# Closing feed-forward, down projection: inner chunks 0 to 7 as four more pairs of seven half products

## What is computed

```python
def swiglu(h, w_gate, w_up, w_down):
    return (jax.nn.silu(h @ w_gate) * (h @ w_up)) @ w_down
...
        h = h + 0.5 * swiglu(rmsnorm(h, ffn2_norm[layer]),
                             ffn2_w_gate[layer], ffn2_w_up[layer], ffn2_w_down[layer])
    return rmsnorm(h, final_norm)
```

## Time and profile before

| | us |
|---|---|
| median of 3 runs | 2114.79 (2113.94 to 2115.39) |
| profiled execution | 2114.31 |
| its span | 2112.5 |
| PE busy in the span | 2100.9 |
| POOL, DVE, ACT busy | 1554.9, 1328.5, 826.3 |

### The profile page before, as it was taken

How to read it: one execution, slowest core, us unless ns; L and a number is a source line. 1 busy time by engine, 2 the same in 40 slices (tenths; PEclk the granted TensorE clock), 3 DMA queues, 4 the chain that set the end, 5 groups by cost and what they waited for, 6 DMA issues and landing times. The chain is left out here.

```text
span 2112.5 us, 36503 instructions
## 1 busy us (share of the span) xinstructions
PE 2100.9 (99%) x13094; PEld 1855.2 (88%) x13094; DVE 1328.5 (63%) x1973; ACT 826.3 (39%) x1570; POOL 1554.9 (74%) x1390
## 2 busy tenths in 40 slices
PE   9999999999999999999999999999999999999998
PEld 7899988888888899998889998886878888999987
DVE  6876796695455577764377666456872746766533
ACT  5255312034223355541245552134362434555312
POOL 7778897667974778888778887785757656788774
PEclk9999999999999999999999999999999999999999
DMA  6333333223331233333223333332322222333332
GB/s 200 114 120 112 100 99 121 90 77 100 125 104 53 95 104 110 106 105 120 93 97 106 112 104 102 98 100 75 105 86 94 80 65 88 112 102 114 100 99 81
DMA packets 115418, 215.05 MB, mean 102 GB/s; under 512 B 12832, under 2 KB 14400, under 8 KB 115008
## 3 DMA queue, kind: packets, MB, share of 16 engines
q1 hardware_dynamic: 111024, 202.03, 29.5%
q10 hardware_dynamic: 4240, 10.99, 1.4%
HBM read 208.77 MB, written 4.19 MB: 101 GB/s over the span
## 5 line engine op out<-in xcount | busy, mean ns | idle before, releaser
L551 POOL TENSOR_TENSOR w_split<-w_raw,w_split 128x512 fp32r<-128x512 f32 (+1 forms) x486 | 671.0, 1381 | 41.3 <-ACT w_split L1834 1.1
L627 PE MATMUL ps<-x,w_split 128*128 128x512 f32 (+1 forms) x1766 | 680.9, 386 | 0.3 <-DVE tg L2248 0.2
L629 PE MATMUL ps<-x,w_split 128*128 128x512 f32 (+1 forms) x1766 | 674.0, 382 | 0.0
L628 PE MATMUL ps<-x,w_split 128*128 128x512 f32 (+1 forms) x1766 | 673.7, 382 | 0.0
L541 POOL TENSOR_SCALAR w_split<-w_raw 128x512 fp32r<-128x512 f32 x482 | 338.0, 701 | 343.5 <-PE ps L629 328.5
L837 PE MATMUL ps<-x,w_split 128*128 128x264 f32 (+1 forms) x1904 | 535.2, 281 | 1.1 <-DVE ps L2351 1.0
L839 PE MATMUL ps<-x,w_split 128*128 128x264 f32 (+1 forms) x1904 | 535.0, 281 | 0.0
L838 PE MATMUL ps<-x,w_split 128*128 128x264 f32 (+1 forms) x1904 | 533.4, 280 | 0.0
L627 PEld LDWEIGHTS ps<-x,w_split 128*128 128x128 f32 x1766 | 331.8, 188 | 74.5 <-issue 9.4
L629 PEld LDWEIGHTS ps<-x,w_split 128*128 128x128 f32 x1766 | 331.9, 188 | 64.6
L628 PEld LDWEIGHTS ps<-x,w_split 128*128 128x128 f32 x1766 | 332.0, 188 | 64.2 <-issue 1.4
(11 more groups left out here) (350 smaller groups left out, 2547.7 us busy)
## 6 DMA issues: line engine op xcount, KB each, us to landing
w_raw<-in_stream SPq DMA_DIRECT2D x758, 256.0 KB, 2.8
arena<-in_memT ACTq DMA_DIRECT2D x2, 1024.0 KB, 5.5
s_tables<-kv ACTq DMA_DIRECT2D x4, 512.0 KB, 3.0
arena<-s_tables ACTq DMA_DIRECT2D x4, 512.0 KB, 4.2
out<-h ACTq DMA_DIRECT2D x6, 256.0 KB, 2.3
h<-in_xT SPq DMA_DIRECT2D x4, 256.0 KB, 5.0
...
```

The costliest lines, as they stand in the source:

```text
L551: pool.tensor_tensor(lo, x, hi.bitcast(F32), ALU.subtract).then_inc(split_ready if half else S("half_split"), 1)
L627: pe.matmul(dst, wh, xh, start=start, stop=False)
L628: pe.matmul(dst, wh, xl, start=False, stop=False)
L629: return pe.matmul(dst, wl, xh, start=False, stop=stop)
```

## The change

Feed-forward 3 gets four more pairs, 22 to 25 (EXTRA = {3: 4}). Pair 22 + j is the product of hidden chunks 0 to 7 with the output tiles 2j and 2j + 1 of the down projection, in the place of a gate and an up tile. The other 14 hidden chunks go through the down projection as before (DOWN_N[3] = 14). The weight stream keeps its 381 blocks; 8 of them are laid out otherwise. The token side of these pairs are hidden chunks: three blocks as they are (A11, and A21 and A22 together in Aa and Ab), and four sums S1, S2, S4, S3, each made in two halves of two chunks, so eight steps (HID_SUMS). In pair 11 + i DVE makes sum i (`hid_add`) and in the next its low part (`hid_sum_low`), ACT its high part (`hid_sum_high`). In pair 21 ACT makes the high parts of A11, Aa and Ab; DVE makes the low parts of A11 and Aa, POOL that of Ab, behind its work for pair 22. DVE adds half of the outputs of these pairs to h at once.

The core of the diff:

```diff
+EXTRA = {3: 4}
+SEVEN_END = {f: FC + EXTRA.get(f, 0) for f in SEVEN}
+SEVEN_BEFORE = {f: sum(SEVEN_END[g] - at for g, at in SEVEN.items() if g < f) for f in range(5)}
+EVICTED_BEFORE = {f: FC * f + sum(n for g, n in EXTRA.items() if g < f) for f in range(5)}
+DOWN_N = {f: FC - 2 * EXTRA.get(f, 0) for f in range(4)}
+HID_SUMS = [f"{name}{u}" for u in "ab" for name in ("S1", "S2", "S4", "S3")]
+HID_PARTS = ["lead"] + HID_SUMS + ["A11", "Aa", "Ab"]
+HID_FROM = 11
...
+            def hid_low(f, name):
+
+                high, src = hid_operand(f, name, 0)
+                pool.wait_ge(S("s_hi"), hid_part(f, name))
+                pool.tensor_tensor(hid_operand(f, name, 1)[0], src, high.bitcast(F32), ALU.subtract
+                                   ).then_inc(S("hid_lo"), 1)
...
-                    for p in range(SEVEN[f], FC):
-                        if p - 2 >= SEVEN[f]:
+                    for p in range(SEVEN[f], SEVEN_END[f]):
+                        if SEVEN[f] <= p - 2 < FC - 2:
                             seven_product(f, p - 2)
+                        if f in EXTRA and p >= FC + 2:
+                            seven_product(f, p - 4)
                         seven_prepare(f, p)
-                    seven_product(f, FC - 2)
-                    b = FFN_AT[f] + 2 * FC
+                        if f in EXTRA and p == FC:
+                            hid_low(f, "Ab")
...
+                if p == FC:
+                    pe.wait_ge(S("s_lo"), hid_lower(f, "A11"))
...
-                with pe.Fori(1, 5) as i:
+                with pe.Fori(1, (nd - 2) // 4) as i:
...
+                def hid_sum_high(i):
+
+                    name, u = HID_SUMS[i][0:2], "ab".index(HID_SUMS[i][2])
+                    act.wait_ge(S("s_sum"), sums_before(f, len(HID_SUMS)) + 4 + i + 1)
+                    act.activation(hid_summed(name, 0, slice(2 * u, 2 * u + 2)), hid_sum, ACT.Copy
+                                   ).then_inc(S("s_hi"), 1)
+
+                def hid_high(name):
+
+                    q = seven_of(f, FC - 1)
+                    act.wait_ge(S("m_done"), 3 * q + (1 if name == "A11" else 3))
+                    dst, src = hid_operand(f, name, 0)
+                    act.activation(dst, src, ACT.Copy).then_inc(S("s_hi"), 1)
+
+                for p in range(at, SEVEN_END[f]):
                     high(p, "T4")
-                    if p > at:
+                    if at < p <= FC:
                         silu((p - 1) // 2, (p - 1) % 2)
-                    more = p + 1 < FC
+                    more = p + 1 < SEVEN_END[f]
                     if p > at:
                         keep(p, "c1")
                     if more:
                         high(p + 1, "B11")
+                    if f in EXTRA and p == HID_FROM - 1:
+                        hid_lead()
+                    if f in EXTRA and HID_FROM <= p < HID_FROM + 8:
+                        hid_sum_high(p - HID_FROM)
                     keep(p, "c5")
+                    if f in EXTRA and p == FC - 1:
+                        hid_high("A11")
                     keep(p, "c2")
+                    if f in EXTRA and p == FC - 1:
+                        hid_high("Aa")
+                        hid_high("Ab")
...
+                    if p >= FC:
+                        out_tile = h[:, 2 * (p - FC) + 1, :]
+                        dve.scalar_tensor_tensor(out_tile, ps[:, BANKS[2 * s + 1], :], 0.5, out_tile, ALU.mult, ALU.add
+                                                 ).then_inc(S("up_ready"), 1)
+                        return
...
+                def hid_add(i):
+
+                    name, u = HID_SUMS[i][0:2], "ab".index(HID_SUMS[i][2])
+                    left, right = {"S1": (hid_quarter(2, 1, u), hid_quarter(2, 2, u)),
+                                   "S2": (hid_sum, hid_quarter(1, 1, u)), "S4": (hid_quarter(1, 2, u), hid_sum),
+                                   "S3": (hid_quarter(1, 1, u), hid_quarter(2, 1, u))}[name]
+                    dve.wait_ge(S("hid_done"), FC * f + 8)
+                    if i:
+                        dve.wait_ge(S("s_lo"), hid_lower(f, HID_SUMS[i - 1]))
+                    dve.tensor_tensor(hid_sum, left, right, ALU.add if name == "S1" else ALU.subtract
+                                      ).then_inc(S("s_sum"), 1)
+
+                def hid_sum_low(i):
+
+                    name, u = HID_SUMS[i][0:2], "ab".index(HID_SUMS[i][2])
+                    chunks = slice(2 * u, 2 * u + 2)
+                    dve.wait_ge(S("s_hi"), hid_part(f, HID_SUMS[i]))
+                    dve.tensor_tensor(hid_summed(name, 1, chunks), hid_sum, hid_summed(name, 0, chunks).bitcast(F32),
+                                      ALU.subtract).then_inc(S("s_lo"), 1)
...
+                def hid_aside(p):
+
+                    if p == HID_FROM:
+                        hid_lead_low()
+                    if HID_FROM < p <= HID_FROM + 8:
+                        hid_sum_low(p - HID_FROM - 1)
+                    if HID_FROM <= p < HID_FROM + 8:
+                        hid_add(p - HID_FROM)
+                    if p == FC:
+                        hid_low("Aa")
```

More of the change, by code:

```diff
@@ L173 @@
 TABLES_BEHIND, SQUARES_BEHIND = (8, 13), 17
-SEVEN_BEFORE = {f: sum(FC - at for g, at in SEVEN.items() if g < f) for f in range(5)}
+EXTRA = {3: 4}
[6 more added lines that the diff above has]
+HID_FROM = 11
 SUMS_AT = {1: "S2", 2: "S4", 3: "S3"}
@@ L253 @@
 A_GAINED = 14 * T
+A_HID = FC * T
 A_QHI = 16 * T
@@ L275, in seven_at, with sums_before @@
     return sorted(SEVEN).index(f)
+def sums_before(f, parts):
+    return 4 * seven_at(f) + sum(parts for g in EXTRA if g < f)
 def is_seven(b):
-    return any(FFN_AT[f] + 2 * at <= b < FFN_AT[f] + 2 * FC for f, at in SEVEN.items())
+    return any(FFN_AT[f] + 2 * at <= b < FFN_AT[f] + 2 * SEVEN_END[f] for f, at in SEVEN.items())
 def sevens_before(b):
@@ L452, in held_chunk, with hid_summed, hid_quarter, hid_operand @@
             return X[1 - NORM_TO[FFN_NORM[f]]][:, SEVEN_HELD[name] + k, part, t]
+        hid_sums = {"S4": kv_r[:].rearrange("p (c s t) -> p c s t", c=4, s=2),
+                    "S1": ar_r[:, A_HID:A_HID + 8 * T].rearrange("p (c s t) -> p c s t", c=4, s=2)}
+        hid_sums["S3"], hid_sums["S2"] = hid_sums["S4"], hid_sums["S1"]
+        hid_sum = ar[:, A_HID + 8 * T:A_HID + 9 * T].rearrange("p (c t) -> p c t", c=2)[:, :, 0:SECOND_T]
+        def hid_summed(name, part, chunks=slice(0, 4)):
+            t = slice(LEAD, FIRST_T) if name in ("S1", "S4") else slice(FIRST_T, T)
+            return hid_sums[name][:, chunks, part, t]
+        def hid_quarter(i, j, u):
+            at = 4 * (j - 1) + 2 * u
+            return hid[:, at:at + 2, FIRST_T if i == 2 else LEAD:T if i == 2 else FIRST_T]
+        def hid_operand(f, name, part):
+            x = NORM_TO[FFN_NORM[f]]
+            if name == "A11":
+                return X[x][:, 0:4, part, 0:FIRST_T], hid[:, 0:4, 0:FIRST_T]
+            at = 4 if name == "Aa" else 6
+            return X[1 - x][:, at:at + 2, part, :], hid[:, at:at + 2, :]
+        def hid_part(f, name):
+            return HID_PARTS.index(name) + 1 + sums_before(f, len(HID_PARTS)) + 4
+        def hid_lower(f, name):
+            return HID_PARTS.index(name) + 1 + sums_before(f, len(HID_PARTS) - 1) + 4
+        def down_chunk(f, d):
+            x = NORM_TO[FFN_NORM[f]]
+            return X[x if f in EXTRA else 1 - x], [6, 7, 4, 5][d % 4]
         block = ctx.enter_context(nc.Block())
@@ L522, in _ @@
                 plain(first, FFN_AT[f] + 2 * SEVEN[f])
-                for p in range(SEVEN[f], FC + 1):
+                for p in range(SEVEN[f], SEVEN_END[f] + 1):
                     seven(f, p)
-                first = FFN_AT[f] + 2 * FC + 2
+                first = FFN_AT[f] + 2 * SEVEN_END[f] + 2
             plain(first, N_BLOCKS)
@@ L1593, in ffn @@
                 else:
-                    with act.Fori(1, 3 if f == 2 else 5) as i:
+                    with act.Fori(d0 // 4 + 1, 3 if f == 2 else 5) as i:
                         for s in range(4):
@@ L2296, in ffn @@
                 else:
-                    with dve.Fori(1, 3 if f == 2 else 5) as i:
+                    with dve.Fori(d0 // 4 + 1, 3 if f == 2 else 5) as i:
                         for s in range(4):
@@ L2410, in seven @@
                 gate((at - 1) // 2, (at - 1) % 2)
-                for p in range(at, FC):
-                    more = p + 1 < FC
+                def hid_add(i):
[8 more added lines that the diff above has]
+                                      ).then_inc(S("s_sum"), 1)
@@ L2416, in seven @@
                     low(p, "T4")
+                    if f in EXTRA:
+                        hid_aside(p)
                     if more:
                         add(p + 1, "T1")
-                    if p == at:
+                    if f in EXTRA and p == FC - 1:
+                        hid_low("A11")
+                        join(p, "C12")
+                        join(p, "C22")
```

(23 more changed lines are left out.)

121 lines of the change are left out of this document (80 added, 41 removed).

## The result

| | before | after |
|---|---|---|
| median, us | 2115.39 (2113.51 to 2116.78, 11 runs) | 2120.02 (2119.31 to 2121.82, 11 runs) |
| profiled execution, us | 2114.31 | 2120.02 |
| its span, us | 2112.5 | 2118.2 |

The ratio is 1.0023, interval 1.0014 to 1.0032: 3.0 to 6.8 us slower, on either side of the 0.2% that a measurement can tell. A second set of runs of the changed kernel (after_again), beside runs of before of its own, gave 1.0023 [1.0014, 1.0032] again. The forecast was 2120.6.

What follows compares the result with a forecast made beforehand. PE, busy 99% of the span, was taken to set the end alone, with any wait added in full. -3.82 (PE's work) + 8.5 (B22) + 1.6 (pair 22) = +6.3 on 2114.3 gave 2120.6 us, own range 2118 to 2123.5.

Steps and rivals of the forecast that it cites:

- PE's work, -3.82: On PE, 8 chunks (43.53 us) go and 4 pairs (39.71 us) come: -3.82 us if PE never waits.
- the estimate: PE's exchange of matmuls by the skill's formula for one matmul alone: 36.8 us for 41.4 us, -4.6 us.
- B22 in pairs 11 to 18, +8.5: PE waits before product B22 for ACT's copy c5: 0.8 us in pair 11, 1.1 in each of 12 to 18.
- the chain: Pairs 11 to 18: DVE's addition waits for POOL's product, ACT's high part and c5 for the addition, B22 for c5.
- Rival A: Pairs 11 to 18: DVE's addition gets in ahead of POOL's product, 0.1 us a pair; 2112.9 us in all, chance 0.17.
- C22 with time to spare: Pairs 11 to 18: DVE's sum C22 ends some 0.8 us before PE's last product needs it, as before.
- Pair 22, +1.6: Copies of hidden chunks and POOL's Ab delay T1's sum; C22 ends at about 10.1, PE wants it at 8.6.
- the prediction's steps for Ab: Pair 22: POOL starts low part Ab at 3.4, about 2.5 us, to 6.9; T1's sum then ends at 7.5.
- they stand ahead of the copies T1, T2, B22, T3, B21, which all slip by some 2.1 us: Pair 21: ACT's three copies of hidden chunks, 3.1 us, delay pair 22's copies by some 2.1 us, and POOL's low parts.
- its base: The forecast adds its +6.3 to 2114.3, the profiled execution of before (2114.31 us); the median is 0.5 above.

Runs made afterwards that it cites:

- e2: Changed kernel, but in pairs 11 to 18 POOL makes the hidden product behind B11's low part, not ahead of it; ratio to before 0.9990 [0.9981, 1.0000].
- e3: Changed kernel, but in pairs 11 to 18 DVE makes the addition first and the sum's low part behind T1's sum; ratio to before 0.9989 [0.9979, 0.9999].
- e1: Changed kernel, but in pairs 11 to 18 ACT makes each hidden sum's high part ahead of copy B21, not c5; ratio to before 0.9999 [0.9989, 1.0008].
- e5: Changed kernel, but in pair 21 ACT's copies Aa and Ab stand behind copies T3 and B21, no longer ahead of T1; one run, 2121.80 us.

## Why the prediction came out

**PE's work, -3.82**: -3.81; the rows' paces held to 0.01. The formula of the Trainium skill's "TensorE: Matmul & The Clock Gate" (Back-to-back issue gap) for a single matmul, by which the estimate was -4.6, is off by 0.8.

**B22 in pairs 11 to 18, +8.5**: +8.34 (0.76 + 7 x 1.083, forecast 0.8 + 7 x 1.1). Each step of the chain stands where it was put. In us from the pair's first matmul (1936.08): product in at 2.11 (forecast 2.12), its end at 3.70 (3.75), the addition's end at 4.23 (4.35), c5's end at 5.16 (5.25), B22 at 5.30 (5.40). The forecast of B22 was late by 0.10, and the 0.08 that the next matmul loses was not in it: two small errors that nearly cancel. e2 and e3 show the cause by taking it away. Rival A was near in its price (0.18 a pair in e2, where the addition gets through; 0.1 forecast) and wrong in its condition: POOL's product does come first.

**C22 with time to spare**: 0.8 us in the forecast. In after it holds; e1 shows that the spare time was there only because B22's wait delayed T4 as well. That sentence was true and less safe than it read.

**Pair 22, +1.6**: +1.69, with the wait and its path as forecast, but the size by luck. T3's low part ends 2.17 into pair 22 (forecast 2.2), Ab holds T1's sum, and C22 is late by it (1.32 us at T4: the step of 1.35 and the 0.08 behind it, less the usual 0.115). The Trainium skill's "SBUF — State Buffer" (SBUF: two separate sides) has the shared port pair held for the whole instruction by whoever starts first; the trace agrees, now for an instruction of that length: T1's sum took 2.45 us and ended 0.56 behind Ab, and came in between where Ab was cut in two.

The luck is in the sum. The prediction lets POOL begin Ab at 3.4, gives it 2.5 us and has it end at 6.9, but 3.4 + 2.5 is 5.9. With 5.9 its own steps bring C22 to 9.1 where PE wants it at 8.6, about +0.6 in the place of +1.6, and the whole to about 2119.6 us, still within its range. In after Ab begins 3.38 into the pair (1991.26 - 1987.88) and ends at 6.75, since it takes 3.37 us. DVE was already at the low part of Aa:

```profile
1990.52 1.86 DVE L2559 TENSOR_TENSOR x<-arena,x 128x1024 fp32r<-128x1024 f32 x1
```

In e5, where Ab came first, it took 2.39. So a slip of 1.0 in the sum stood in for a wait of 0.98 behind an instruction of DVE that the prediction's steps for Ab don't name.

The step "they stand ahead of the copies T1, T2, B22, T3, B21, which all slip by some 2.1 us" was only half of the cause. ACT and DVE by time in pair 21 (from 1977.96) of after:

```profile
1982.74 2.00 ACT L1781 ACTIVATE x<-arena 128x1024 fp32r<-128x1024 f32 x2
1984.63 0.59 ACT L1722 ACTIVATE w_split<-ps 128x512 fp32r<-128x512 f32 x1
...
1985.26 0.42 DVE L2456 TENSOR_TENSOR ps<-ps,sq 128x248 f32<-128x248 f32 x1
1985.59 0.69 DVE L2434 TENSOR_TENSOR ps<-w_raw,ps 128x512 f32<-128x512 f32 x1
```

Behind Aa and Ab T1's copy starts 6.67 in, where it does so 4.79 in in pair 17 of before: a slip of 1.88. It ends at 1985.22, and T2's sum, which in before starts 0.13 behind that copy, could have begun at 1985.35. But on DVE it stands behind C22 and begins at 1985.59, a slip of 2.12. Two causes end 0.24 us apart. Either alone would make nearly all of the slip: e5 shows it for DVE's order; for the copies alone it is worked out from these rows, and no run shows it. So the forecast of 2.1 from one of them fitted. DVE's order in pair 21 is part of the change, and the prediction left it out; e5, which took the named cause away and gained nothing, brought it to light. Not foreseen either was the 0.37 us at T2 of pair 22: c1 stands behind a silu that waits for DVE's late gate tile.

**The end**: 6.3 forecast, 6.57 by PE's rows; 5.7 by the spans, and 4.6 between the medians, whose interval holds both. That 2120.6 lies only 0.6 from the measured 2120.02 is in part luck again: its base, the profiled 2114.31, is 1.1 below the median of before, and the shorter end of after takes back about as much. No run ties either to the change.
